# The last expert row moves from TensorE to VectorE, and the last tile's final norm is shared by three engines

## The reference, cut to what matters

```python
def rms_norm(x, w):
    y = xf * lax.rsqrt(jnp.mean(xf * xf, axis=-1, keepdims=True) + EPS)
    return (y * w.astype(jnp.float32)).astype(x.dtype)

def eval_block(args):                      # in peer(): 128 tokens at a time
    xb, ib, gb = args                      # tokens, expert numbers, gates
    u = expert_down[ib]
    pre = jnp.einsum('bthkd,btd->bthk', u, xb).astype(f32)
    act = (jax.nn.gelu(pre, approximate=False) * gb).astype(xb.dtype)
    return jnp.einsum('bthk,bthkd->btd', act, expert_up[ib])

h = h + hybrid_mixer(rms_norm(h, norm_mix[l]), ...)      # in reference()
h = h + peer(rms_norm(h, norm_ffn[l]), ...)
return rms_norm(h, norm_final)
```

## Time and profile before

| | us |
|---|---|
| median of 3 runs | 1527.85 |
| lowest and highest | 1527.29 and 1528.53 |
| the profiled execution, its time | 1526.34 |
| its span, first to last instruction | 1524.5 |

### The profile page before, as it was taken

How to read it: one execution, slowest core, us unless ns; L and a number is a source line. 1 busy time by engine, 2 the same in 40 slices (tenths; PEclk the granted TensorE clock), 3 DMA queues, 4 the chain that set the end, 5 groups by cost and what they waited for, 6 DMA issues and landing times.

```text
span 1524.5 us, 14446 instructions
## 1 busy us (share of the span) xinstructions
PE 1325.1 (87%) x4392; PEld 678.5 (45%) x4392; DVE 1053.0 (69%) x2534; ACT 441.6 (29%) x1216; POOL 1108.3 (73%) x1005
## 2 busy tenths in 40 slices
PE   8999998899888998889889898889888878888886
PEld 5557974444444443444444443434444334434432
DVE  3546598886776777677766676777777676667664
ACT  2123462122323232233223222233233222222222
POOL 0001134548899898888999998888999888888893
PEclk9999999999999999999999999999999999999999
DMA  7640069999999999999999999999999999999995
GB/s 254 172 184 12 1 259 413 412 418 422 421 420 422 421 421 422 421 421 421 421 421 418 421 416 422 422 421 409 408 421 423 420 422 422 421 421 421 416 415 231
DMA packets 85217, 569.80 MB, mean 374 GB/s; under 512 B 10227, under 2 KB 12564, under 8 KB 18708
## 3 DMA queue, kind: packets, MB, share of 16 engines
q0 software_dynamic: 73728, 536.90, 85.1%
q1 hardware_dynamic: 11412, 31.99, 6.2%
HBM read 565.19 MB, written 3.67 MB: 373 GB/s over the span
## 4 chain that ended last, share of the span: by engine, by line
DMA 32%; PE 30%; POOL 21%; DVE 10%; issue 4%; ACT 3%; SPq 0%; DVEq 0%; ACTq 0%; POOLq 0%
DMA arena<-in_experts_du_dram,arena 27%; PE ps L1477 14%; POOL arena L419 11%; POOL arena L409 8%; PE ps L1245 5%; DMA wide<-in_experts_du_dram,arena 5%; PE ps L1416 3%; DVE arena L1053 3%; PE ps L1451 3%; POOL wide L409 2%; ACT arena L647 1%; DVE wide L1053 1%; ACT arena L468 1%; PE ps L1260 1%; PE ps L1232 1%
## 5 line engine op out<-in xcount | busy, mean ns | idle before, releaser
L1477 PE MATMUL ps<-arena 128*128 128x512 f32 x1624 | 774.7, 621 | 141.6 <-ACT arena L647 133.0
L409 POOL DMA_INDIRECT arena<-in_experts_du_dram,arena x418 | 488.0, 1168 | 120.1 <-issue 63.8
L1477 PEld LDWEIGHTS ps<-arena 128*128 128x128 f32 x1624 | 307.3, 196 | 565.7 <-issue 329.9
L419 POOL TENSOR_SCALAR arena<-ident,arena 128x128 f32<-128x128 f32 x464 | 494.8, 1066 | 47.5 <-PE ps L1477 31.9
L1053 DVE CUSTOM_DVE_ANT_0 arena<-arena,wide 128x1024 f32<-128x1024 f32 x210 | 255.3, 1229 | 138.3 <-DMA arena<-in_experts_du_dram,arena 137.5
L1053 DVE CUSTOM_DVE_ANT_0 arena<-arena 128x1024 f32<-128x1024 f32 x208 | 252.6, 1228 | 114.8 <-DMA arena<-in_experts_du_dram,arena 114.1
L643 ACT ACTIVATE arena<-arena 128x2 f32<-128x2 f32 (+1 forms) x234 | 47.5, 203 | 762.0 <-DVE arena L1053 761.7
L1477 PE MATMUL ps<-wide,arena 128*128 128x512 f32 x376 | 183.2, 610 | 29.8 <-ACT arena L647 26.1
L647 ACT ACTIVATE arena<-arena 128x128 f32<-128x128 f32 x464 | 161.1, 394 | 8.1 <-ACT arena L643 0.2
L409 POOL DMA_INDIRECT wide<-in_experts_du_dram,arena x94 | 107.5, 1144 | 60.9 <-DVE arena L1037 24.0
L1477 PEld LDWEIGHTS ps<-wide,arena 128*128 128x128 f32 x376 | 70.0, 194 | 124.8 <-issue 73.6
(11 more groups left out here) (197 smaller groups left out, 1028.4 us busy)
## 6 DMA issues: line engine op xcount, KB each, us to landing
arena<-in_w_in_blocks_dram SPq DMA_DIRECT2D x16, 512.0 KB, 9.5
arena<-in_experts_du_dram,arena POOLq DMA_INDIRECT x418, 16.4
wide<-in_w_query_dram SPq DMA_DIRECT2D x5, 1024.0 KB, 9.3
wide<-in_w_out_dram SPq DMA_DIRECT2D x1, 4096.0 KB, 17.8
h<-in_x_dram SPq DMA_DIRECT2D x4, 512.0 KB, 9.7
arena<-in_w_query_dram SPq DMA_DIRECT2D x2, 1024.0 KB, 6.4
arena<-in_x_t_dram SPq DMA_DIRECT2D x3, 512.0 KB, 6.5
line_scratch<-arena SPq DMA_DIRECT2D x1, 1536.0 KB
```

Of the source, the lines that this page charges most:

```text
L409: gp.indirect_dma_start(rows[b], None, experts_du, bass.IndirectOffsetOnAxis(ap=idx[:, (q // PH) % 2, q % PH * TOPK + i:q % PH * TOPK + i ...
L419: g.tensor_scalar(diag(s), ident[:], eg[:, q % 2, i:i + 1], None, ALU.mult).then_inc(sem("gate_diag"), 1)
L1477: last = mm(acc(t, b)[:], diag(s), up[:, b * 512:(b + 1) * 512], start=(s % SLOTS == 0), stop=False, skip_group_check=True)
```

## The change

- TensorE leaves out slot 511, GpSimd leaves out its gate diagonal, and ScalarE only takes its Gelu.
- VectorE (`last_finish`) multiplies that Gelu value by its gate, waits until TensorE is through with slot 510, and adds up half times that value to each half of `acc`, into `xn2[1]` in SBUF.
- The squares: half 0 on ScalarE (from SBUF), half 1 on VectorE by the custom instruction of the dots, with 512 columns.
- GpSimd multiplies half 1 by the final weights, into the free down half of slot 510's row. ScalarE then scales this product by the reciprocal root; VectorE finishes half 0 as before.
- The Sqrt on ones stands right behind the last Gelu. The store of half 1 waits for ScalarE's `last_scaled`.

```diff
@@ sync
-                    sp.wait_ge(sem("final_ready"), 2 * t + b + 1)
+                    if 2 * t + b == 2 * NT - 1:
+                        sp.wait_ge(sem("last_scaled"), 1)
+                    else:
+                        sp.wait_ge(sem("final_ready"), 2 * t + b + 1)
@@ gpsimd
-            gate_diagonal(NS - 1)
+            gp.wait_ge(sem("last_sum"), 2)
+            gp.wait_ge(sem("row_free"), PE_DONE[NS - 2])
+            link(gp, g.tensor_tensor(rows[ROW_OF[NS - 2]][:, 0:512], xn2[1][:, 512:], w_late[:, 512:], ALU.mult),
+                 "last_weighted", n)
@@ scalar, late_group
-                for s in range(s0, s0 + n_slots):
+                for s in range(s0, min(s0 + n_slots, NS - 1)):
@@ scalar, in place of final_squares(NT - 1)
+            def last_squares():
+                nc.scalar.activation(ss[:, 14:15], ones[:, 0:1], ACT.Sqrt).then_inc(sem("root_ready"), 1)
+                act.wait_ge(sem("last_sum"), 1)
+                copy(rows[ROW_OF[NS - 1]][:, 0:512], xn2[1][:, 0:512], "fin_sq", ACT.Square, accum_out=ss[:, 12:13])
+                act.wait_ge(sem("mean_sq"), 1)
+                nc.scalar.activation(ss[:, 14:15], ss[:, 14:15], ACT.Sqrt, scale=1.0 / D).then_inc(sem("fin_root"), 1)
+                act.wait_ge(sem("last_weighted"), 1)
+                act.wait_ge(sem("last_factor"), 1)
+                nc.scalar.activation(xn2[1][:, 512:], rows[ROW_OF[NS - 2]][:, 0:512], ACT.Copy, scale=ss[:, 15:16]
+                                     ).then_inc(sem("last_scaled"), 1)
@@ vector, in place of finish(NT - 1)
+            def last_finish():
+                s, t = NS - 1, NT - 1
+                col = slice(s % 16, s % 16 + 1)
+                final = xn2[t % 2]
+                dve.wait_ge(sem("gelu"), N_BEFORE[s] + 1)
+                go(v.tensor_tensor(actv[:, col], gel[:, col], eg[:, (NQ - 1) % 2, col], ALU.mult))
+                dve.wait_ge(sem("row_free"), PE_DONE[s - 1])
+                for b in range(2):
+                    half = slice(512 * b, 512 * b + 512)
+                    go(v.scalar_tensor_tensor(final[:, half], rows[ROW_OF[s]][:, D + 512 * b:D + 512 * b + 512],
+                                              actv[:, col], acc(t, b)[:], ALU.mult, ALU.add), "last_sum")
+                go(v.tensor_tensor_reduce(rows[ROW_OF[s]][:, 512:D], final[:, 512:], final[:, 512:], 1.0, 0.0, ALU.mult,
+                                          ALU.add, ss[:, 13:14]))
+                dve.wait_ge(sem("fin_sq"), 2 * t + 1)
+                dve.wait_ge(sem("root_ready"), 1)
+                go(v.scalar_tensor_tensor(ss[:, 14:15], ss[:, 12:13], D * EPS, ss[:, 13:14], ALU.add, ALU.add), "mean_sq")
+                dve.wait_ge(sem("fin_root"), 1)
+                go(v.reciprocal(ss[:, 15:16], ss[:, 14:15]), "last_factor")
+                go(v.scalar_tensor_tensor(final[:, 0:512], final[:, 0:512], ss[:, 15:16], w_late[:, 0:512], ALU.mult, ALU.mult),
+                   "final_ready")
@@ tensor
-                    if not by_dve(s):
+                    if not by_dve(s) and s < NS - 1:
```

More of the change, by code:

```diff
@@ L650, in final_squares @@
             def final_squares(t):
-                if t == NT - 1:
-                    nc.scalar.activation(ss[:, 14:15], ones[:, 0:1], ACT.Sqrt).then_inc(sem("root_ready"), 1)
                 act.wait_ge(sem("acc_half"), t + 1)
@@ L656, in final_squares @@
                 copy(xn2[t % 2][:, 512:], acc(t, 1)[:], "fin_sq", ACT.Square, accum_out=ss[:, 13:14])
-                if t == NT - 1:
-                    act.wait_ge(sem("mean_sq"), 1)
-                    nc.scalar.activation(ss[:, 14:15], ss[:, 14:15], ACT.Sqrt, scale=1.0 / D).then_inc(sem("fin_root"), 1)
+            def last_squares():
[8 more added lines that the diff above has]
+                                     ).then_inc(sem("last_scaled"), 1)
             dt_exps()
@@ L767, in _ @@
                             transposed(t + 1, 1)
-            final_squares(NT - 1)
+            last_squares()
         @block.vector
@@ L1077, in finish @@
                 final = xn2[t % 2]
-                if t + 1 < NT:
-                    dve.wait_ge(sem("late_w"), 4 * t + 4)
+                dve.wait_ge(sem("late_w"), 4 * t + 4)
                 dve.wait_ge(sem("fin_sq"), 2 * t + 2)
[L1081 to L1088, removed]
+                go(v.tensor_tensor(ss[:, 14:15], ss[:, 12:13], ss[:, 13:14], ALU.add))
+                rms(ss[:, 15:16], ss[:, 14:15], 1.0 / D, "dve_step")
                 for b in range(2):
@@ L1216, in _ @@
                             norm_ffn_tile(t + 1, w_late)
-            finish(NT - 1)
+            last_finish()
         @block.tensor
```

## The result

| | kernel before | changed kernel |
|---|---|---|
| median, 13 runs each | 1527.03 us | 1530.5 us |
| lowest and highest | 1524.69 and 1529.94 | 1529.19 and 1532.76 |
| ratio, with its 95% interval | | 1.0027 (1.0019 to 1.0034) |
| the profiled execution's span | 1524.5 | 1531.0 |
| start of the last dot | 1514.43 | 1516.88 |

What follows compares the result with a forecast made beforehand. The prediction held that gathers bound the kernel to 1514.4 us, leaving only a 10.1 us tail to move; its terms netted -0.05 us on the second store, 1527.85 - 0.05 = 1527.8 us, range 1526.0 to 1528.9.

Steps and rivals of the forecast that it cites:

- 1: On ScalarE the Sqrt load follows Gelu's end (1515.90) at once; its Sqrt ends at 1517.4, 0.44 us earlier.
- 2: VectorE's gate product ends at about 1516.15; TensorE is done with slot 510 by 1516.02.
- 5: GpSimd's product of half 1 with the weights is held by VectorE's squares until 1518.45 and ends at 1519.58.
- step 6: `mean_sq` on VectorE falls into GpSimd's product and ends with it at 1519.61: +0.26 us in place of -0.7.
- 7: Root, reciprocal and half 0 end 1.55 us behind `mean_sq`, as before: half 0 at 1521.16, its store issued at 1521.18.
- step 8: ScalarE scales half 1 from 1520.27 to 1521.0, ready before half 0; GpSimd's product is not what it waits for.
- 9: The second store follows the first at once, issued at 1521.66 instead of 1521.71; data end at 1523.2 to 1523.3.
- The sum: Terms removed from and added to the tail's path: net -0.05 us on the second store, median 1527.8 us.
- B: Rival in the tail: no collision on `mean_sq`, which ends 0.71 us earlier at best; time 1526.8 us, chance 0.20.
- C: Rival in the tail: GpSimd's product gets ahead of VectorE's squares or exceeds 1.27 us; time 1528.1 us, chance 0.16.
- A: The forecast itself: GpSimd's product and `mean_sq` collide, the tail is a wash; 1527.8 us, chance 0.58.
- D: Rival ahead of the tail: the gathers' 1514 us drift between programs, either sign; chance 0.06.

Runs made afterwards that it cites:

- e4: The changed kernel with an extra GpSimd drain behind its last gate diagonal, ahead of its wait for the tail: 1526.01 us, ratio 0.9992.
- e1: The changed kernel with the block closed without GpSimd's drain: 1526.94 us against 1527.28, ratio 0.9999.
- e3: The kernel before with a one-column GpSimd memset added in the tail, once the two sums of squares are added: 1531.36 us, ratio 1.0024.

## Why the prediction was wrong

By its own steps:

1. Gelu to load: 1518.35 to 1518.37, right.
2. Gate product 0.16, end 0.20 after Gelu's end (forecast 0.25), right. The wait for slot 510 cost nothing.
3. The sums 1.53, right.
4. Squares on VectorE 0.69, right to the hundredth.
5. Product held, 1.76 from its start and done 5.07 us after the last dot's start; forecast 1519.58 - 1514.43 = 5.15. Right. The Trainium skill's rule (SBUF — State Buffer, section Who interferes with whom) holds here with the earlier trace rows: e4 shows both instructions short where they don't meet. One of my rows was weaker than I took it for: when the one-column operation at 200.57 began, GpSimd was still issuing a gather (200.15 to 201.30), so the product from 201.34 on can't be all that held it. That a product holds a one-column operation is shown by step 6.
6. `mean_sq` with the product's end: 1.09, right.
7. From the end of `mean_sq` to that of half 0 1.35 (1521.97 to 1523.32), forecast 1.55: too long by 0.2. In the kernel before half 0 started 0.23 behind the reciprocal, in the changed kernel 0.04. Half 0 now reads SBUF in place of PSUM and in another shape; which of the two it is was not tested.
8. Half 1 on ScalarE ends at 1523.35, 0.03 behind half 0 on VectorE. I had it end ahead of it, so this sign failed; it costs nothing, since the second store is issued later still.
9. The stores are 0.4 apart, forecast 0.5. The second is issued 6.8 us after the last dot's start, where it was 7.3 before and I had 7.2. From issue to landing the two take 2.2 us (median), before 2.0, so most of what the issue gained is lost again: SyncE's branch is 0.1 earlier than before.

The sum behind these steps, -0.05 us, is right for SyncE's branch (-0.1) and, at the second store's issue, off by 0.4: that the two nearly agree at the end is luck, a stretch taken 0.2 too long and a landing taken too short. The terms listed under "The sum" don't add up to it either: the two squares on ScalarE, which leave the path (1.4 us), and the second store's issue, which joins it (0.5), are missing there; the -0.05 comes from the steps' times. None of this is the miss. **The step that failed is the one ahead of them, where I read GpSimd as idle**: "in the last ten microseconds ... GpSimd does nothing at all", and step 8, which asks of the product only when it is ready for ScalarE ("The product itself (1519.58) is not what it waits for"). What GpSimd still has to do behind the product stands in the sum at nothing, without a reason. Busy time doesn't count a drain. GpSimd wasn't idle before: its drain ran until 1518.5 under the last gathers and the tail, and the change took its cover away. The forecast took the second store for the end of the program in both kernels. In the kernel before it is; behind the product the end is at 1522.0 + 0.5 + 8.3, 4.5 us beyond SyncE.

The term missing in the sum is therefore +4.0 us from last dot to end of span (14.1 against 10.1). The medians give 3.5, the ratio 4.1 with an interval of 2.9 to 5.2 us.

The rivals: B and C were about the collision and both wrong on it; the collision came as in A. C had the right sign for the wrong cause, with 0.3 us where 4 were due. D, a shift ahead of the tail: its sign did show, a last dot at 1516.88 in the one profile. As the cause it is excluded by e1, which runs the same gathers and the same tail and is as fast as before, and by e3, which has the loss without the change. What I should have asked is what follows the last store: which engine closes the block last, and what of that was hidden. The trace of the kernel before had it (line 99, a drain of 18.2 us), and the same rule that I held to for instructions, to name what hides a cost of nothing, goes for the end of the program as well.

## What to carry to other kernels

Before you give the last stretch of a program work on an engine that was done early, look up what that engine still does after its last instruction, in the sequencer's rows of the block's end and not in busy time. A GpSimd that issued many gathers owes a drain that grows with their number, in these runs by 11.6 to 16.0 ns for each gather of 1 MB; keep its last instruction early enough to hide it, drain early where it idles anyway, or close the block without the drain where every gather has been waited for. Count the tail from an instruction that both kernels share, since a microsecond there shows in one pair of profiles (whose own ends differ by up to 0.3), while the intervals of the ratios here are some 1.3 us to either side.

## What the runs showed of the hardware that I had not expected

- GpSimd's drain at the end of a block costs 8.3 us behind 512 gathers that have all landed, 3.1 behind 256 and 1.7 behind 128 (4 buffers), 0.16 behind none, 0.04 right after an earlier drain. The Trainium skill (VectorE: DVE Perf Modes, section The DRAIN you can't avoid) gives the drains that frame a kernel as about 12 ns, constant and on all engines. Of SyncE (7 ns) and VectorE (17 ns) the trace agrees; of GpSimd it does not, and the measurement decides. TensorE's (2.03 us) and ScalarE's (0.21 before, 0.73 in the changed kernel) are longer too, but each begins with its engine's last instructions and lasts as long as they do (1.98, 0.20 and 0.72).
- On VectorE a one-column sum with two SBUF inputs takes 0.16 alone and 1.09 beside a GpSimd product; the scaling of half 0, 512 columns with two SBUF inputs, 0.75 and 1.32.
- A Sqrt's table load of 1.28 (1518.37 to 1519.65) lay under VectorE's gate product and two sums (1518.39 to 1520.11): moving slot 511's row to VectorE took both the diagonal and the load off the path.
